# Sample attention in pairs and column groups, rope keys by fours, a turned down product, norms on VectorE, and later weights in a one-core decoder step

## The reference

```
# sample attention, 8 samples, 16 heads, 1024 past keys each in 8 pages of 128
q_lat  = einsum('bqhd,rhd->bqhr', q_nope, w_uk)              # 256 wide
s_past = einsum('bqhr,bkr->bhqk', q_lat, ckv_past) + einsum('bqhe,bke->bhqk', q_rope, kr_past)
s_new  = the same with the sample's own key
p      = softmax(concat([s_past, s_new]) * ATTN_SCALE)
o_lat  = einsum('bhqk,bkr->bqhr', p[..., :past], ckv_past) + the own key's part
out    = einsum('bqhr,rhd->bqhd', o_lat, w_uv)
# experts, d_model 1024, d_expert 512
h = silu(t @ w_gate[e]) * (t @ w_up[e]);  y = sum_e combine[e] * (h @ w_down[e])
# after every sub-layer
x = layer_norm(ALPHA * x + f(x)) * g + b
```

## Time and profile before

| | us |
|---|---|
| median of three runs | 1211.73 |
| profiled execution, device time | 1213.42 |
| its span, first to last instruction | 1211.7 |
| PE busy | 1054.5 (87%) |
| DVE busy | 370.1 (31%) |
| output product and norms of the prompt (242 to 315) | 73 |
| sample attention (315.6 to 425.1) | 109.5 |
| from there to the first expert tile (425.1 to 476.3) | 51 |
| expert stage of layer 0 (476.3 to 762.3) | 286 |
| from its end to the next expert tile (762.3 to 884.5) | 122 |
| expert stage of layer 1 (884.5 to 1171.1) | 287 |
| end (1171.1 to 1211.7) | 41 |

### The profile page before, as it was taken

The page is one execution under the profiler, slowest core; times in us unless marked ns, Lnnn a source line. Parts: engine busy times, 40 slices in busy tenths (PEclk is TensorE's granted clock), DMA queues, the critical chain, the costliest instruction groups (busy, mean ns, idle before and its releaser), DMA issues.

```text
span 1211.7 us, 28356 instructions
## 1 busy us (share of the span) xinstructions
PE 1054.5 (87%) x11923; PEld 740.8 (61%) x11923; DVE 370.1 (31%) x798; ACT 194.0 (16%) x428; POOL 111.2 (9%) x184
## 2 busy tenths in 40 slices
PE   7899999899899932999999999178189999999985
PEld 6677777544444322677677668067067776776752
DVE  1334444322433251111111111497511111111117
ACT  1234444400222112000000000131020000000000
POOL 0001001030033103000000000321300000000012
PEclk9999999899999965999999999677589999999997
DMA  9324335230023097999999999606359999999915
GB/s 342 146 86 133 106 112 178 82 79 1 1 78 92 26 392 274 350 384 392 395 385 394 397 389 392 215 3 246 141 200 387 386 395 391 387 400 389 377 51 201
DMA packets 80864, 296.04 MB, mean 244 GB/s; under 512 B 10184, under 2 KB 41168, under 8 KB 72495
## 3 DMA queue, kind: packets, MB, share of 16 engines
q1 hardware_dynamic: 53351, 247.50, 54.5%
q10 hardware_dynamic: 19712, 26.75, 6.5%
q0 software_dynamic: 7760, 21.24, 5.1%
HBM read 255.80 MB, written 40.11 MB: 244 GB/s over the span
## 4 chain that ended last, share of the span: by engine, by line
PE 83%; DVE 7%; DMA 4%; POOL 2%; issue 2%; ACT 2%; ACTq 0%; SPq 0%; POOLq 0%; DVEq 0%
PE PS L896 19%; PE PS L874 15%; PE PS L884 14%; PE PS L801 5%; PE PS L573 4%; PE PS L738 4%; PE PS L620 3%; PE PS L636 3%; PE PS L761 2%; PE PS L529 2%; PE PS L629 2%; PE PS L719 2%; PE PS L551 2%; POOL expert_rows L1036 2%; PE PS L806 1%
## 5 line engine op out<-in xcount | busy, mean ns | idle before, releaser
L896 PE MATMUL PS<-ring,arena 128*96 128x512 f32 x512 | 227.4, 597 | 0.0
L874 PE MATMUL PS<-arena,ring 128*64 128x96 f32 x4096 | 180.5, 250 | 53.5 <-DVE arena L1649 53.5
L874 PEld LDWEIGHTS PS<-arena,ring 128*64 128x64 f32 x4096 | 174.4, 140 | 77.4 <-issue 77.4
L884 PE MATMUL PS<-arena,ring 128*64 128x96 f32 x4096 | 174.4, 246 | 0.0
L884 PEld LDWEIGHTS PS<-arena,ring 128*64 128x64 f32 x4096 | 170.9, 137 | 0.0
L896 PEld LDWEIGHTS PS<-ring,arena 128*96 128x96 f32 x512 | 80.8, 163 | 123.0 <-issue 119.2
L1649 DVE STREAM_TRANSPOSE arena<-arena 128x768 uint32<-128x768 uint32 x34 | 54.2, 1593 | 206.7 <-ACT arena L1227 176.6
L1669 DVE COPY arena<-PS 96x512 f32<-96x512 f32 x32 | 22.0, 687 | 218.0 <-PE PS L896 218.0
L1231 ACT ACTIVATE arena<-PS 96x512 f32<-96x512 f32 x32 | 19.0, 593 | 379.3 <-PE PS L896 379.3
L801 PE MATMUL PS<-ring,arena 128*128 128x512 f32 x128 | 55.7, 594 | 0.7 <-issue 0.7
L1002 POOL DMA_DIRECT2D ring<-cache_krope x64 | 34.6, 541 | 141.3 <-issue 141.3
(11 more groups left out here) (245 smaller groups left out, 1061.2 us busy)
## 6 DMA issues: line engine op xcount, KB each, us to landing
ring<-w_gate SPq DMA_DIRECT2D x32, 2048.0 KB, 15.2
ring<-w_up SPq DMA_DIRECT2D x32, 2048.0 KB, 15.9
ring<-w_down SPq DMA_DIRECT2D x32, 2048.0 KB, 16.3
arena<-expert_rows ACTq DMA_DIRECT2D x144, 96.0 KB, 9.6
expert_out<-arena ACTq DMA_DIRECT2D x32, 384.0 KB, 8.3
expert_rows<-ring SPq DMA_DIRECT2D x6, 1920.0 KB, 10.1
ring<-cache_ckv SPq DMA_DIRECT2D x64, 128.0 KB, 2.1
ring<-w_o SPq DMA_DIRECT2D x1, 4096.0 KB, 19.3
```

The lines of the kernel that those rows point to most:

```text
L874: last = nc.tensor.matmul(bank(s, KF, CAP)[at:at + 64, f, :], wg[w][:, k, P * f + at:P * f + at + 64], xeT[s][:, k, :], start=(k == 0), st ...
L884: last = nc.tensor.matmul(out[at:at + 64, :], wu[w][:, k, P * f + at:P * f + at + 64], xeT[s][:, k, :], start=(k == 0), stop=(k == KD - 1))
L896: last = nc.tensor.matmul(bank(4 + hf)[0:CAP, :], h[s][:, f, :], wd[w][:, f, 512 * hf:512 * (hf + 1)], start=(f == 0), stop=(f == KF - 1))
```

## The change

Seven parts; everything else is as before.

1. Samples go two at a time (`BATCHES` = 4 pairs), in four column groups of 32: group g holds the 16 heads of sample g % 2 and keys 512 (g // 2) to 512 (g // 2) + 511. Scores, new keys and weighing each issue four matmuls of 32 stationary columns, one a group. The softmax is over 128 partitions x 520 columns; minimum and sum are joined across the two halves of partitions by small DVE operations. The latent is summed over the halves by a matmul with a constant (`fold2`).
2. Rope keys of four pages lie side by side in 128 columns and are turned by one transpose. The queries' rope part is laid out with zeros (`qz`), four copies made by one matmul (`fold4`) and four DVE copies. So 36 transposes for two samples stand where 48 did.
3. Keys are loaded by POOL during and after the prompt's attention; pages of pairs 0 to 2 by SP after it, those of pair 3 by SP and POOL once pair 0 is weighed.
4. The down product has 64 weight columns stationary and 96 columns of h moving, as gate and up have. Its result has the model's columns on partitions, is copied to `yT`, and turned back by eight transposes (`turn_back`) in the next tile, after the first quarter of its gate product. Copies and store follow there. After the last tile comes one more turn.
5. The second norm of layer 0 is done on DVE alone, as the first was (`norm`), in place of ACT, DVE and POOL.
6. The first weights of layer 1 (slot 1) are loaded after all gathers have landed.
7. The constants are cut to the size held; the last 192 columns are loaded later.

```
-            def sample(b, s, before, after_one, following):
+            def score_pages(u):
+                pe.wait_ge(tp_ev[0], 5 * u + 5)
+                pe.wait_ge(tp_ev[1], 5 * u + 5)
+                pe.wait_ge(qb_set, u + 1)
+                for c in range(MKV):
+                    for g in range(4):
+                        nc.tensor.matmul(bank(0)[32 * g:32 * g + 32, :], qb[u % 2][:, c, g % 2, :],
+                                         kpT[g % 2][c][:, 512 * (g // 2):512 * (g // 2 + 1)], start=(c == 0), stop=False)
+                for a in range(4):
+                    for g in range(4):
+                        nc.tensor.matmul(bank(0, 4, P)[32 * g:32 * g + 32, a, :], qz[:, 2 * u + g % 2, a, :],
+                                         krT[g % 2][:, g // 2, :], start=False, stop=(a == 3))
...
+            def weigh_pages(u):
+                pe.wait_ge(spT_ev, u + 1)
...
+                for a in range(4):
+                    for g in range(4):
+                        last = nc.tensor.matmul(bank(7, KVL)[32 * g:32 * g + 32, :], psT_s[:, a, 32 * g:32 * g + 32],
+                                                ckp[u % 3][g % 2][:, 4 * (g // 2) + a, :], start=(a == 0), stop=(a == 3 and g >= 2))
...
+                for u in range(BATCHES):
+                    score_pages(u)
+                    if u:
+                        weigh_pages(u - 1)
+                    if u < BATCHES - 1:
+                        turn_pages(u + 1)
+                    if u:
+                        turn_latent_out(u - 1)
+                    pe.wait_ge(sexp_set, u + 1)
+                    for a in range(4):
+                        nc.tensor.transpose(bank(2, 4, P)[:, a, :], ps_s[:, P * a:P * (a + 1)], ident)
...
+            def sample_pair(u):
+                first, second = slice(0, 64), slice(64, P)
+                if u < BATCHES - 1:
+                    set_qb(u + 1)
+                dve.wait_ge(sc_ps, u + 1)
+                link(v.tensor_tensor(bank(1, DB), bank(1, DB), own_sample[:, u, :], ALU.add))
+                link(v.tensor_reduce(s_min, view(PS, 0, 512 + DB), AXX, ALU.min))
+                link(v.tensor_copy(s_other[first, :], s_min[second, :]))
+                link(v.tensor_tensor(s_mneg[first, :], s_min[first, :], s_other[first, :], ALU.min))
+                v.tensor_copy(s_mneg[second, :], s_mneg[first, :]).then_inc(smin_set, 1)
...
             def samples():
+                v.memset(qz, 0.0)
+                v.memset(qb[0], 0.0)
+                link(v.memset(qb[1], 0.0))
```

```
+                def turn_back(tl):
+                    pe.wait_ge(q["yT_set"], 2 * tl + 2)
+                    for m in range(KD):
+                        last = nc.tensor.transpose(bank(4 + m // 4, 4, P)[0:CAP, m % 4, :], yT[:, m, :], ident)
+                    last.then_inc(q["back_ps"], 1)
...
                     for f in range(KF):
+                        if f == 1:
+                            turn_back(tl)
...
+                    def down(m, blocks):
+                        for f in blocks:
+                            for at in (0, 64):
+                                last = nc.tensor.matmul(bank(4 + m // 4, 4, CAP)[at:at + 64, m % 4, :],
+                                                        wd[w][:, f, P * m + at:P * m + at + 64], h[s][:, f, :],
                                                         start=(f == 0), stop=(f == KF - 1))
...
+                    down(0, range(KF - 1))
+                    down(4, range(KF - 1))
+                    pe.wait_ge(q["h_set"], 2 * tl + 2)
+                    down(0, (KF - 1,))
+                    down(4, (KF - 1,))
+                    for m in (1, 2, 3, 5, 6, 7):
+                        last = down(m, range(KF))
...
-                    load_expert(1, 0, 1, (S[0]["gate_ps"][0], nh), (S[0]["up_ps"][0], 2 * nh), (S[0]["down_ps"][0], nh))
...
+                    for slot, rows in ((0, 64), (1, 64), (2, 32)):
+                        sp.wait_ge(gath[slot], rows)
+                    load_expert(1, 0, 1, (S[0]["gate_ps"][0], nh), (S[0]["up_ps"][0], 2 * nh), (S[0]["down_ps"][0], 2 * nh))
...
             for step in range(NT + 4):
                 if step < NT:
-                    stats(0, 1, step)
-                if 2 <= step <= NT:
-                    gain(0, step - 1)
-                if step < NT:
-                    spread(0, step)
-                if step == 0:
-                    gain(0, 0)
+                    norm(0, 1, step)
                 if step >= 4:
                     if step - 4 == 3:
                         dve.wait_ge(pool_out, 32)
-                    norm1(1, step - 4)
+                    norm(1, 0, step - 4)
```

More of the change, by code:

```diff
@@ L22 @@
 PAST = PAGE * NPAGES
+BATCHES = DB // 2
+LATE = P + 64
 E, GROUPS, EPG, F = 16, 4, 4, 512
@@ L85, in constants @@
     put("causal", np.concatenate([np.zeros((P, SEQ - P)), np.where(i[None, :] > i[:, None], BIG, 0.0)], 1))
-    put("own_sample", np.broadcast_to(np.where(np.eye(DB) > 0, 0.0, BIG)[None], (H, DB, DB)))
+    own = np.full((P, BATCHES, DB), BIG)
+    for u in range(BATCHES):
+        for ab in range(2):
+            own[32 * ab:32 * ab + 32, u, 2 * u + ab] = 0.0
+    put("own_sample", own)
     band = np.zeros((P, 2, 4, BAND), np.float32)
@@ L1073, in _ @@
                 gather(3)
-                for i in range(NT):
+                if L == 0:
+                    gather(4)
+                for i in range(NT if L else 0):
                     shift(L, i)
@@ L1211, in experts @@
                 act.sem_inc(q["y_set"], 1)
+                for s in range(2):
+                    act.sem_inc(q["y_st"][s], 16)
                 act.wait_ge(scat, 160 * (L + 1))
@@ L1218, in experts, with store, tile @@
                     nc.scalar.activation(X[0:n, i, :], X[0:n, i, :], ACT.Copy, scale=ALPHA).then_inc(xscaled, 1)
-                def tile(u, s, stored):
+                def store(tl, s, count):
+                    act.wait_ge(q["back_ps"], tl + 2)
+                    act.wait_ge(q["y_st"][s], count)
+                    nc.scalar.activation(ys[s][0:CAP, 0:512], bank(4)[0:CAP, :], ACT.Copy).then_inc(q["y_set"], 1)
+                    act.wait_ge(q["y_set"], 2 * tl + 4)
+                    act.dma_start(yd[bass.ds(CAP * tl, CAP), :], ys[s][0:CAP, :]).then_inc(q["y_st"][s], 16)
+                def tile(u, s, more):
                     tl = 2 * u + s
@@ L1260, in samples, with take_pages @@
-            def samples():
-                sample(0, False, True)
-                with act.Fori(1, DB - 1) as b:
-                    sample(b, True, True)
-                sample(DB - 1, True, False)
-                take_latent_out(DB - 1)
+                store(2 * nh - 1, 1, 16 * nh)
+            def take_pages(u):
+                for n in range(1, 10, 2):
+                    act.wait_ge(tp_ps, 10 * u + n + 1)
+                    if n < 8:
+                        ab, c, hf = n // 4, n // 2 % 2, n % 2
+                        ins = nc.scalar.activation(kpT[ab][c][:, 512 * hf:512 * (hf + 1)], bank(page_bank[(10 * u + n) % 3]), ACT.Copy)
+                    else:
+                        ins = nc.scalar.activation(krT[n - 8], bank(page_bank[(10 * u + n) % 3], 2, P), ACT.Copy)
+                    ins.then_inc(tp_ev[1], 1)
```

379 lines of the change are left out of this document (186 added, 193 removed).

## The result

The changed kernel takes 1183.01 us (median of four runs, 1179.35 to 1187.23) against 1213.47 for the kernel before on the same chip (1211.29 to 1215.57): a ratio of 0.975 with a 95% interval of 0.971 to 0.980. The forecast was 1130 us with a range of 1116 to 1157, so of some 82 us only 30 came. The profiled execution took 1180.57 us, with a span of 1178.8.

The account below looks back on a forecast made before the run. PE was taken to bound the kernel (83% of the chain), with DMA engines full too. Samples 58.4, down product 18.9, last turning -1.8 and between stages 6.6 cut 82.1 us from the 1211.7 span: 1130 us, range 1116 to 1157.

Parts of the forecast that it names:

- Its 64 weights and 96 columns are the up product's: Expert tile: the turned down product takes 5.28 us in place of 7.04, like the up product.
- Everything is covered: Expert tile: copies, bank releases and ACT's loads and store finish in time, so no waits replace the 18.9 us gain.
- Samples: Samples in pairs: 46.8 us instead of 109.5; with 4.3 lost ahead of them, a gain of 58.4 us.
- the bound from the earlier trace: Samples: if small records cost 0.05 us, rope and own keys are 1.3 us a pair dearer, 5 in all.
- The rival of groups that run one after another: Samples: the four column groups don't run side by side, 13.2 us more a pair, 53 in all: 1183 us; chance 5%.
- Ahead of them: Before the samples: memsets and query copies 2.9 us, two more rounds of page copies 1.4; 4.3 us lost.
- The tile: Expert tile: three products, turning and changes of form take 17.16 us, 0.59 less; 18.9 us over 32 tiles.
- the clock rival: Expert tile: PE stops at each turning for yT and its clock falls, 3.6 us a tile: 1245 us; chance 2%.
- Weights: Expert loop: down weights land 0.8 us later each tile, to some 25 us; 3.2 us of slack remain, no wait.
- The first rival: Expert loop: weights bind, a tile's transfers needing 18.6 us at 380 GB/s; 5 us a layer, 1140 us; chance 10%.
- Between the stages: Between the expert stages: earlier store and gather and the norm on DVE alone gain 6.6 us, layer 0's turning included.
- The end: After layer 1's last tile: the last turning and its copy in a row cost 1.8 us.

Follow-up runs that it names:

- e1: 40 increments of a semaphore nobody waits for on PE ahead of layer 1's expert loop, added to the changed kernel; 1134.61 us, ratio 0.935.
- e6: e1 with the last pair's page numbers read ahead of the wait and three memsets moved before the fourth tile's norm; 1132.12 us, ratio 0.936.
- e4: The kernel before with the turned down product alone; 1202.15 us, ratio 0.989.
- e8: e1 with layer 1's first three weight loads issued as before the change, ahead of layer 0's last stores and gathers; 1139.86 us, ratio 0.941.
- e7: e1 with layer 0's second norm split over DVE, ACT and POOL again, as before the change; 1141.98 us, ratio 0.942.
- e3: The changed kernel with the down product of the kernel before, all else kept; 1150.23 us, ratio 0.946.
- e9: e1 with 16 increments ahead of layer 1's loop instead of 40; 1136.20 us in one run.
- e10: e1 with 200 increments ahead of layer 1's loop instead of 40; 1143.18 us in one run.
- e2: The changed kernel with 80 such idle increments on PE ahead of layer 0's expert loop and none ahead of layer 1's; 1183.16 us.
- e11: e1 with 232 increments ahead of layer 1's loop instead of 40; 1192.77 us in one run.

## Why the prediction was wrong, step by step

**The step that failed** is the one that costed the turned down product: "Its 64 weights and 96 columns are the up product's". That holds for the time of a product and was taken for all that it costs. It also makes the loop 480 instructions longer, and where the loop of layer 1 lay, PE stood three times for its own instructions. Each time cost 16.5 us with its aftermath, and the stage takes 324.4 us where it takes 275.8 without them (e1) and the forecast had 277.2. The step "Everything is covered" looked at copies and banks alone, and neither this part, nor the rivals, nor the list of what would make the prediction wrong asked where instructions come from. The page's 27 packets were there to be read, and so were the two loops of 1,100 instructions, which had four packets each in their first pass and afterwards a single one, at 758 us, in layer 0's last pass. Without the misplaced loop (e1) the sum stands: a span of 1129.9 against the forecast 1129.6. That it is so close is luck, as its terms err in both directions:

- *Samples.* Forecast 46.8 us, 46.2 after, 44.4 in e1. The middle pair takes 10.8 instead of 11.5 (e6): scores 1.85 + 0.86 + 0.18 for 3.3, weighing 1.79 + 0.55 for 2.3, pages 4.12 + 0.44 for 4.4, latent 0.39, probabilities 0.44 + 0.11. These rows fill the period, so the 0.6 for changes between groups and the whole array isn't there, and small records didn't cost more: the bound from the earlier trace rows wasn't needed. The Trainium skill, TensorEngine Tiling (Array Packing), section "Tiling Modes", has such a change drain TensorE; at four column groups and back several times a pair, these rows leave little room for it: they fill the period to 0.05 us, and the scores, the weighing and the page turns are together 0.13 us longer than costed by their records (1.76, 1.76, 4.11). The rival of groups that run one after another (53 us) is refuted: L781 in e1, eight groups of 256 columns, takes 1.78 us as costed. That this rival's 1183 us is the time measured is chance. The wait for the third pair's pages was put at 1.3 and measured 1.78 after, 1.54 in e1.
- *Ahead of them.* Forecast 4.3 us. From the fourth tile's norm to the first score it was 12.2 us before (the norm's first row is the one here, the score in the earlier trace rows):

```profile
303.32 1.22 DVE L1483 SCALAR_TENSOR_TENSOR X<-X,PS 128x1024 f32<-128x1024 f32 x1 [11.02 <-PE PS L801]
```

  It is 18.1 in e1 and 18.8 after, 5.9 and 6.6 more; the page turns there run at a clock of 0.50 to 0.74 in the changed kernel (26 records in 5.82 us where 34 take 4.12 later in e6). That was not in the sum. e6 wins 3.0 back.
- *The tile.* Forecast 17.16, measured 17.00: turning 1.01 for 0.97, but only one of two changes of form costs 0.15. 32 x 0.75 would be 24 us; the stages of e1 give 7.8 + 10.8 = 18.6, near the forecast 18.9 by two errors that cancel: in the first two tiles of a stage, where the longer loop is fetched for the first time, e1 needs 38.6 and 37.8 us for 34.0 where the kernel before needed 37.4 and 38.1 for 35.5, which is 3.9 of the 5.4 us that are missing, and at the end of layer 0 weights are late by 1.1 (next point). After has three "issue" gaps there in layer 0, of 0.35, 1.53 and 0.89 us. No wait of PE for yT was seen, so the clock rival (1245) falls.
- *Weights.* Forecast: landing grows by 0.8 us a tile to 25, slack 3.2 us. In e1 it grows from 14.0 (issued 472.70) to 29.9 (issued 659.70), 11 tiles on, 1.45 a tile: 0.16 of that because a tile is shorter than costed, the rest because the transfers reach 380 to 391 GB/s and not 392 throughout. The load before the last lands at 642.70 + 28.9 = 671.6 and its product starts at 671.73, 0.35 us after PE was free. The last load lands at 659.70 + 29.9 = 689.6, and its product starts at 689.68 after a wait:

```profile
689.68 5.50 PE L941 MATMUL PS<-arena,ring 128*64 128x96 f32 x128 [0.73 <-DVE arena L1750]
```

  DVE had been done before, at 689.25. So the slack is used up, and the waits are for weights. The first rival's rate was nearly right (18.45 us a tile against its 18.6), and its price 1.1 us in layer 0 and none in layer 1 instead of 5 in each. In the changed kernel the down weights issued from 1000 to 1100 us land after 13.7 us, since the stops let them catch up, against 25.4 in e1.
- *Between the stages.* Forecast 115.6, measured 117.1 and 116.4. The first addition comes 13.2 us after the last product in e1 and not 11.6. From e4's 124.2 us, which include the turning but neither move, the norm alone takes off 4.5 (e8; forecast 4.2) and the late weights another 3.3 beside it (forecast 4.2 for store and gather, of which the turning takes 1.8 back). Without the norm's move the late weights give nothing (e7): its chain runs over PE's products for the pooling mixer from 733.69 us on, as the chain of before does from 798.22 on, so that an earlier first addition doesn't bring the end forward. The forecast added the two as if each stood alone; the sum came out right because both were made.
- *The end.* Forecast 1.8 us longer; 0.6 after, 1.9 in e1.

## What to carry to other kernels

When a change replaces few wide instructions by many narrow ones in a hardware loop, count the engine's instructions in a pass and where the loop lies, and look at the instruction queue's packets: their number on the page against the length of the engine's list, and in windows of the DMA view, where the loops that ran well here moved none between their first and their last pass. Where an "issue" gap stands at a loop's jump back, put idle instructions ahead of the loop: if the gap goes or changes and the packets fall, it was a fetch. And take each part alone as well: e3 is some 30 us faster than the full change, which alone would have pointed at the product, while 16 idle instructions (e9) were the better answer.

## What the hardware showed that I had not expected

- PE's loop is kept while it touches seven stretches of 256 instructions (e1, e9, e10, e2's layer 1) and is fetched again when it touches eight (after, e2's layer 0, e11), with the borders where the stops put them; position alone makes 48 us of difference. The Trainium skill, Runtime: NRT & Kernel Launch, section "Instruction fetch mechanics", gives TensorE 2048 instructions, that is eight blocks; by that eight stretches should just stay, and the runs show that they don't. What becomes of the eighth is open. The same section speaks of two lines only; by that every loop here would be fetched on each pass, and the 27 packets of before contradict it.
- A jump back to a stretch that isn't held costs 12.1 us with 2 MB loads in flight, 7.4 to 8.4 with 1 MB and 6.2 to 7.1 with few bytes, and then about 4 us more at half clock and in short stops.
- In profiled executions whose programs are the same up to the first expert tile, that tile starts anywhere from 417.0 (e1) to 421.9 us (e3), so differences below 5 us between single executions are read by stage.
